# Transposes of the next chunk's keys and values placed between the state products of an mLSTM chunk on TensorE

## The chip, the cores and the metric

The kernel runs on one core of one Trainium2 chip. The metric is the device time of one execution in microseconds. Each of the runs shown is one execution on that core; the median of the runs is what a change is judged by.

## What is computed

A decoder trunk of two layers is run once, for a prompt group (16 meta tokens and 1024 prompt tokens) and a sample group (8 sequences of 4 tokens). Layer 0 is sliding-window attention, layer 1 an mLSTM block; both groups share the weights. The part that matters here is the chunkwise mLSTM cell of layer 1, for 4 heads of width 512. Per head and chunk the reference does this:

```
b = jnp.cumsum(fc, axis=1)
...
s = jnp.einsum('bthd,bjhd->btjh', qc, kc) * w_intra
num = jnp.einsum('btjh,bjhd->bthd', s, vc) + w_inter[..., None] * jnp.einsum('bthd,bhde->bthe', qc, C)
den = jnp.sum(s, axis=2) + w_inter * jnp.einsum('bthd,bhd->bth', qc, n)
h = num / jnp.maximum(jnp.abs(den), jnp.exp(-m_t))[..., None]
...
C_new = decay[..., None, None] * C + jnp.einsum('bjhd,bjhe->bhde', kc * wk[..., None], vc)
n_new = decay[..., None] * n + jnp.einsum('bjh,bjhd->bhd', wk, kc)
```

`s` are the scores of a chunk, `num` the numerator, `C` the 512x512 state and `n` the sum of keys. Outputs are the trunk's outputs and all new states, among them the 512x512 state of each head for the prompt and for each of the 8 sample sequences.

## The kernel before

The program has two blocks. The first does layer 0 and the projections of layer 1, and leaves queries, keys, values and two gate tensors in HBM (`scratch_q`, `scratch_k`, `scratch_v`, `scratch_ga`, `scratch_gb`). The second block (from about 1514 us of the span on) is the cell and the output projection, and holds the change. Each engine has its own program, in which the order is the order of the code; the engines meet in semaphores alone.

**Loops.** Each engine runs the four heads in turn. A head has 9 prompt chunks, c = 0 to 8: chunk 0 is the 16 meta tokens, the others have 128 tokens. The 8 sample sequences are taken along: iteration c of the chunk loop also does the state update of sequence c - 2. Behind the loop stand the last sequence, the samples' outputs and the output projection (L1813), and between its tiles the entry of the next head (its sample chunk and its chunk 0).

**An iteration on TensorE** (`cell_pe`, L1759 to L1797) has this order:

1. numerator and denominator from the old state (L1770, L1773), with the four state updates of sample sequence c - 2 between them (L1706), then the chunk's own part of both (L1776, L1781);
2. the state products: four products of keys and values, k = 0 to 3, each of three matmuls of 512 columns (high and low parts, L1788), which alternate between two PSUM banks. Product k waits until VectorE has added product k - 2 to the state (L2053, `c_done`);
3. `pre(c + 1)`: it waits until the next chunk's queries, keys and values have landed (`wait_chunk`) and until the two PSUM banks `KT_` and `VT_` are free, turns the keys (4 transposes) and the values (4 transposes; L1679), and multiplies keys and queries to scores (L1685);
4. the sample numerator of sequence c - 1 (L1716), and the transposes of chunk c's normed output (`back`, L1697), which wait for ScalarE (L1912).

VectorE has, in an iteration, the statistics of the numerator's rows (L2017), and between its small steps the four additions to the state (L2053), then the weighting of the next scores (L1961). ScalarE norms the output of chunk c (L1905 to L1912) before it copies the turned keys and values of chunk c + 1 out of PSUM (L1881, L1883). GpSimd scales the next chunk's queries (L1587), for which it too waits until the chunk has landed, and prepares the sample keys (L1605).

**Loads and stores** are all issued by SP, in one queue, in the order of `cell_sp` (L1541 to L1550). A chunk's three tensors (256 KB each) go into one of two buffers `chin`, which the next chunk but one uses again. From iteration 2 on the queue runs through this cycle, for b = c - 2:

```
            if b + 3 < NP:
                chunk_load(sp, h, b + 3)
                chunk_weights(sp, h, b + 3)
            sp.wait_ge(sem("c_done"), due(NU * h + u_samp(b, 3) + 1))
            sp.dma_start(state(o["sample_mlstm_c"], b), scs[b % 2][:, :, :]).then_inc(sem(f"sc_out{b % 2}"), 16)
            if b + 2 < DECB:
                state_load(b + 2)
            if b + 3 < NP:
                chunk_gates(sp, h, b + 3)
```

`state_load` waits until the store just issued (1 MB) has landed, since it loads the next sequence's state (1 MB) into the same buffer. Behind it come the gates (2 x 256 KB), and then the queries, keys and values of chunk c + 2. These are the ones that TensorE turns in iteration c + 1.

Of the kernel before, what the change touches and what calls it, by code (L numbers as in the profile page):

```python
# [42 lines left out]
P = 128  # L43
# [13 lines left out]
SR = 3 * NSM  # L57
# [31 lines left out]
def due(n):  # L89

    n = n.v if isinstance(n, Idx) else n
    return max(n, 0) if isinstance(n, int) else n
# [31 lines left out]
def build(nc, a, o):  # L124
# [3 lines left out]
    def sem(name):  # L128
        if name not in sems:
            sems[name] = nc.alloc_semaphore(name + sem_suffix[0])  # L130
        return sems[name]
# [22 lines left out]
    ident = const("ident", [P, P])  # L154
# [126 lines left out]
    NCH = NBLK + 2  # L281
# [22 lines left out]
    kv3 = rbuf("kv3", [P, 2, 4, SR])  # L304
# [1096 lines left out]
    NP = NBLK + 1  # L1401
# [34 lines left out]
    def pre_no(c):  # L1436

        return 0 if c == NCH - 1 else c + 1
# [9 lines left out]
    def chunk_in(c):  # L1448
        return smin if c == NCH - 1 else chin[c % 2]
# [5 lines left out]
    def wait_chunk(eng, h, c):  # L1455
        if c == NCH - 1:
            eng.wait_ge(sem("smin"), 144 * h + 144)
        else:
            eng.wait_ge(sem(f"chin{c % 2}"), due(48 * turn_of(h, c) + 48))
# [203 lines left out]
            cell_gp(gp, h + 1, entry=True)()  # L1663

    def cell_pe(pe, h, entry=False):
        def pre(c):

            n, x = ROWN[c], chunk_in(c)
            sample = c == NCH - 1
            wait_chunk(pe, h, c)  # L1670
            pe.wait_ge(sem("kv_ev"), due(2 * NCH * h + 2 * pre_no(c)))
            if c == 0:
                pe.wait_ge(sem("k3_lo"), 2 * h + 2)
            else:
                pe.wait_ge(sem("kv_lo"), due(2 * NP * h + (0 if sample else 2 * c)))
            for i, bank in ((1, KT_), (2, VT_)):
                for k in range(4):
                    src = kv3[:, i - 1, k, :] if sample else x[:, i, k, 0:n]
                    last = pe.transpose(bank[0:SR if sample else n, k * P:(k + 1) * P], src, ident[:, :])  # L1679
                last.then_inc(sem("kv_t"), 1)  # L1680
            pe.wait_ge(sem("sw_done"), due(NCH * h + pre_no(c)))
            pe.wait_ge(sem("small_read"), due(NZ * h + (c + 1 if 0 < c < NCH - 1 else 0)))
            for k in range(4):
                keys = kv3[:, 0, k, :] if sample else x[:, 1, k, 0:n]
                last = pe.matmul(score_bank(c)[0:SR if sample else n, 0:n], keys, x[:, 0, k, 0:n], start=(k == 0), stop=(k == 3))  # L1685
            last.then_inc(sem("s_done"), 1)
# [72 lines left out]
        for c in range(NP):  # L1759
            n, r = ROWN[c], c % 2  # L1760

            pe.wait_ge(sem("sw_done"), due(NCH * h + pre_no(c) + 1))
            wait_apart(pe, sem("kv_ev"), 2 * NCH * h + 2 * pre_no(c) + 2)
            pe.wait_ge(sem("h_done"), due(NCH * h + c))
            small(c + 1)
            if c > 0:
                pe.wait_ge(sem("qs_ready"), due(NCH * h + pre_no(c) + 1))
                pe.wait_ge(sem("c_done"), due(NU * h + u_tile(c - 1, 3) + 1))
                for k in range(4):
                    pe.matmul(pm[0][0:n, :], qs[r][:, k, 0:n], cst[:, k, :], start=(k == 0), stop=False)  # L1770
                    if k == 0:
                        pe.wait_ge(sem("nst_done"), due(NP * h + c))
                    pe.matmul(SM[0:n, 0:1], qs[r][:, k, 0:n], nst[:, k:k + 1], start=(k == 0), stop=False)  # L1773
                    if c > 1:
                        sample_update(c - 2, k)
            pe.matmul(SM[0:n, 0:1], swb[r][0:n, 0:n], ones[0:n, 0:1], start=(c == 0), stop=True)  # L1776
            wait_apart(pe, sem("sw_hi"), NP * h + c + 1)
            wait_apart(pe, sem("sw_lo"), NP * h + c + 1)
            wait_apart(pe, sem("kv_lo"), 2 * NP * h + 2 * c + 1)
            for i, (w, v) in enumerate(((swh, vh), (swh, vl), (swl, vh))):  # L1780
                last = pe.matmul(pm[0][0:n, :], w[r][0:n, 0:n], v[r][0:n, :], start=(c == 0 and i == 0), stop=(i == 2))  # L1781
            last.then_inc(sem("small_ready"), 1)
            pe.wait_ge(sem("kv_lo"), due(2 * NP * h + 2 * c + 2))
            for k in range(4):
                u = u_tile(c, k)
                pe.wait_ge(sem("c_done"), due(NU * h + u - 1))
                for i, (w, v) in enumerate(((kh, vh), (kh, vl), (kl, vh))):
                    last = pe.matmul(U_[u % 2], w[r][0:n, k * P:(k + 1) * P], v[r][0:n, :], start=(i == 0), stop=(i == 2))  # L1788
                last.then_inc(sem("u_ready"), 1)
            if c + 1 < NP:  # L1790
                pre(c + 1)
            if c >= 1:
                sample_numerator(c - 1)
            if c == NP - 1:
                for k in range(4):
                    sample_update(DECB - 1, k)
            back(c)  # L1797
# [939 lines left out]
```

## Time and profile before

| what | us |
|---|---|
| median of 3 runs | 2267.84 |
| lowest and highest of them | 2266.93, 2269.08 |
| the profiled execution, its own time | 2262.78 |
| its span | 2261.0 |
| TensorE busy in it | 2133.8 (94%) |
| VectorE, ScalarE, GpSimd busy in it | 1049.9, 768.1, 486.7 |
| mean granted clock of TensorE | 0.971 |

The span is the time from the first to the last instruction of the program; 1.8 us of the execution lie around it. The profiled execution is 5.1 us shorter than the median of the runs. Busy shares are means over stages that differ: the chunk loop of the cell, where the change is, takes about 105 us in each of the four heads, and only its own rows tell what ends which wait there. Matmuls are pipelined: a row's duration reaches from its start to its end, and the pitch from one start to the next is what it costs in a stream.

### The profile page before, as it was taken

How to read it: one execution, taken by the hardware profiler on the slowest of the kernel's cores; microseconds unless marked ns; L12 is line 12 of the kernel's file. 1: busy time of each engine (PE TensorE's matmuls, PEld its weight loads, DVE VectorE, ACT ScalarE, POOL GpSimd, SP SyncE). 2: the span in 40 equal slices, each digit the busy share in tenths (PEclk: the TensorE clock that was granted, in tenths of full speed). 3: DMA queues.
4: the chain of work that ended last, by engine and by line, in shares of the span. 5: the costliest groups of instructions: out<-in, count | busy, mean ns of one | idle time of the engine just before them, and what ended most of it. 6: DMA issues, size and time to landing. Idle time of an engine off the chain costs nothing. (4 is left out here: it accounts for less than half of the span.)

```text
span 2261.0 us, 32879 instructions
## 1 busy us (share of the span) xinstructions
PE 2133.8 (94%) x13089; PEld 1872.3 (83%) x13089; DVE 1049.9 (46%) x1843; ACT 768.1 (34%) x1609; POOL 486.7 (22%) x479
## 2 busy tenths in 40 slices
PE   4999979998999999999999999985989989989998
PEld 4999977777999989998999899974668668668668
DVE  6222247845645305431543054315753753753762
ACT  3114658843333222332323232313422421421431
POOL 3000015632420001000100010001531531531540
PEclk8999989999999999999999999996999999999999
DMA  6631122013631332233223322228764764664772
GB/s 220 76 88 38 38 58 71 1 32 119 177 88 60 113 125 68 67 115 122 62 66 121 120 61 69 105 80 236 241 190 142 223 207 143 208 215 130 216 226 79
DMA packets 321886, 272.20 MB, mean 120 GB/s; under 512 B 57958, under 2 KB 268454, under 8 KB 321651
## 3 DMA queue, kind: packets, MB, share of 16 engines
q1 hardware_dynamic: 307854, 221.58, 33.2%
q10 hardware_dynamic: 13880, 48.52, 6.6%
q8 instruction: 105, 1.72, 0.3%
q14 instruction: 47, 0.39, 0.1%
HBM read 168.89 MB, written 102.11 MB: 120 GB/s over the span
## 5 line engine op out<-in xcount | busy, mean ns | idle before, releaser
L369 ACT ACTIVATE sb_whi<-sb_wraw 128x1024 fp32r<-128x1024 f32 x108 | 114.1, 1058 | 455.5 <-PE ps L390 379.8
L374 DVE TENSOR_TENSOR sb_wlo<-sb_wraw,sb_whi 128x1024 fp32r<-128x1024 f32 x108 | 140.0, 1297 | 270.1 <-ACT sb_whi L369 263.8
L390 PE MATMUL ps<-sb_h1h,sb_whi 128*128 128x358 f32 x1152 | 252.9, 327 | 0.0
L390 PE MATMUL ps<-sb_h1h,sb_wlo 128*128 128x358 f32 x1152 | 252.8, 327 | 0.0
L390 PE MATMUL ps<-sb_h1l,sb_whi 128*128 128x358 f32 x1152 | 251.4, 326 | 0.0
L390 PEld LDWEIGHTS ps<-sb_h1h,sb_whi 128*128 128x128 f32 x1152 | 199.0, 189 | 2.0 <-issue 1.8
L390 PEld LDWEIGHTS ps<-sb_h1l,sb_whi 128*128 128x128 f32 x1152 | 199.2, 189 | 0.0
L390 PEld LDWEIGHTS ps<-sb_h1h,sb_wlo 128*128 128x128 f32 x1152 | 199.1, 189 | 0.0
L1049 POOL COPY sb_ctail<-sb_xr 128x3 f32<-128x3 f32 x16 | 3.0, 186 | 698.2 <-DVE sb_xr L1182 698.2
L1770 PE MATMUL pm<-sb_cst,sb_qs 128*128 128x512 f32 x256 | 133.4, 603 | 0.1
L390 PE MATMUL ps<-sb_hh,sb_whi 128*128 128x358 f32 x480 | 116.7, 352 | 15.8 <-DVE sb_hl L412 12.6
L1155 ACT ACTIVATE sb_st<-ps 128x1074 f32<-128x1074 f32 x48 | 51.2, 1067 | 222.7 <-PE ps L390 222.7
L1813 PE MATMUL ps<-sb_uh,sb_whi 128*128 128x358 f32 x384 | 93.6, 339 | 18.2 <-POOL sb_ul L1620 18.2
L390 PE MATMUL ps<-sb_hh,sb_wlo 128*128 128x358 f32 x480 | 107.3, 332 | 0.0
L390 PE MATMUL ps<-sb_hl,sb_whi 128*128 128x358 f32 x480 | 107.1, 332 | 0.0
L1976 DVE SCALAR_TENSOR_TENSOR sb_scs<-sb_scs,sb_hbc,ps 128x512 f32<-128x512 f32 x128 | 94.1, 742 | 26.7 <-PE ps L1706 26.7
L390 PEld LDWEIGHTS ps<-sb_hh,sb_whi 128*128 128x128 f32 x480 | 85.5, 194 | 24.7 <-issue 9.6
L1773 PEld LDWEIGHTS ps<-sb_nst,sb_qs 128*128 128x128 f32 x256 | 48.6, 190 | 62.2 <-issue 62.2
L2053 DVE SCALAR_TENSOR_TENSOR sb_cst<-sb_cst,sb_hbc,ps 128x512 f32<-128x512 f32 x128 | 91.8, 741 | 0.0
L1813 PE MATMUL ps<-sb_ul,sb_whi 128*128 128x358 f32 x384 | 91.0, 332 | 0.0
L1813 PE MATMUL ps<-sb_uh,sb_wlo 128*128 128x358 f32 x384 | 90.7, 332 | 0.0
L2176 DVE TENSOR_TENSOR sb_x1T<-ps,sb_x1T 128x1074 f32<-128x1074 f32 x32 | 40.9, 1277 | 104.5 <-PE ps L1813 104.5
(398 smaller groups left out, 4669.4 us busy)
## 6 DMA issues: line engine op xcount, KB each, us to landing
sb_scs<-state_mlstm_c SPq DMA_DIRECT2D x32, 1024.0 KB, 5.7
sample_mlstm_c<-sb_scs SPq DMA_DIRECT2D x32, 1024.0 KB, 4.9
sb_wraw<-mlstm_w_in SPq DMA_DIRECT2D x48, 512.0 KB, 3.9
sb_wraw<-swa_w_in SPq DMA_DIRECT2D x20, 512.0 KB, 3.8
scratch_ga<-sb_st ACTq DMA_DIRECT2D x16, 537.0 KB, 2.9
scratch_gb<-sb_st ACTq DMA_DIRECT2D x16, 537.0 KB, 4.3
scratch_v<-sb_st ACTq DMA_DIRECT2D x16, 537.0 KB, 2.9
scratch_q<-sb_st ACTq DMA_DIRECT2D x16, 537.0 KB, 2.8
```

What stands on the lines that cost most here:

```text
L369: act.activation(whi[q][:, :], wraw[q][:, :], ACT.Copy).then_inc(sem("w_hi"), 1)
L374: dve.tensor_tensor(wlo[q][:, :], wraw[q][:, :], whi[q][:, :].bitcast(F32), ALU.subtract)\
L390: last = pe.matmul(ps[s][:, g, 0:GRP], w[:, kk, c * P:(c + 1) * P], x[:, kk, g * GRP:(g + 1) * GRP], start=(kk == 0 and i == 0), stop=(kk ...
L1049: gp.tensor_copy(dst[:, 0:CW - 1], x[:, NPR:XPR])
L1155: act.activation(v3(st[b][:, 0, :]), ps[c][:, :, 0:GRP], ACT.Copy, scale=(MD ** -0.5 if i // 4 == 2 else 1.0)).then_inc(sem("qkv_ev"), 1)
L1770: pe.matmul(pm[0][0:n, :], qs[r][:, k, 0:n], cst[:, k, :], start=(k == 0), stop=False)
L1773: pe.matmul(SM[0:n, 0:1], qs[r][:, k, 0:n], nst[:, k:k + 1], start=(k == 0), stop=False)
L1813: last = pe.matmul(ps[i % 2][:, g, 0:GRP], w[:, k, c * P:(c + 1) * P], x[:, k, g * GRP:(g + 1) * GRP], start=(k == 0 and t == 0), stop=(k ...
L1976: dve.scalar_tensor_tensor(scs[b % 2][:, k, :], scs[b % 2][:, k, :], hbc[:, 1, NP + b:NP + b + 1], U_[u % 2], ALU.mult, ALU.add).then_inc( ...
L2053: ins = dve.scalar_tensor_tensor(cst[:, k, :], cst[:, k, :], hbc[:, 1, c:c + 1], U, ALU.mult, ALU.add)
L2176: dve.tensor_tensor(v3(x1T[:, i, :]), ps[i % 2][:, :, 0:GRP], v3(x1T[:, i, :]), ALU.add).then_inc(sem("o_done"), 1)
```

## The change

`pre` is taken apart into `turn(c, i)`, which turns the keys (i = 1) or the values (i = 2) of chunk c, and `multiply(c)`, the scores. `turn(c, 1)` carries the waits that stood at the head of `pre`: the one for the chunk's landing, and those for the two PSUM banks. In the chunk loop, the keys of chunk c + 1 are turned behind state product k = 1 of chunk c, its values behind product k = 2, and its scores follow product k = 3. The entry of a head (sample chunk and chunk 0) keeps its order. No instruction is added or taken away on any engine, and the code of the other engines is the same.

```diff
     def cell_pe(pe, h, entry=False):
+        def turn(c, i):
+
+            n, x, bank = ROWN[c], chunk_in(c), (KT_, VT_)[i - 1]
+            sample = c == NCH - 1
+            if i == 1:
+                wait_chunk(pe, h, c)
+                pe.wait_ge(sem("kv_ev"), due(2 * NCH * h + 2 * pre_no(c)))
+                if c == 0:
+                    pe.wait_ge(sem("k3_lo"), 2 * h + 2)
+                else:
+                    pe.wait_ge(sem("kv_lo"), due(2 * NP * h + (0 if sample else 2 * c)))
+            for k in range(4):
+                src = kv3[:, i - 1, k, :] if sample else x[:, i, k, 0:n]
+                last = pe.transpose(bank[0:SR if sample else n, k * P:(k + 1) * P], src, ident[:, :])
+            last.then_inc(sem("kv_t"), 1)
+
         def pre(c):
+
+            turn(c, 1)
+            turn(c, 2)
+            multiply(c)
+
+        def multiply(c):
...
@@ -1787,8 +1798,10 @@
                 for i, (w, v) in enumerate(((kh, vh), (kh, vl), (kl, vh))):
                     last = pe.matmul(U_[u % 2], w[r][0:n, k * P:(k + 1) * P], v[r][0:n, :], start=(i == 0), stop=(i == 2))
                 last.then_inc(sem("u_ready"), 1)
+                if c + 1 < NP and k in (1, 2):
+                    turn(c + 1, k)
             if c + 1 < NP:
-                pre(c + 1)
+                multiply(c + 1)
             if c >= 1:
                 sample_numerator(c - 1)
```

On TensorE, behind the numerator of an iteration, this is the order before (L1781 numerator, L1788 state products, L1679 transposes, L1685 scores, L1716 sample numerator):

```order
L1781 MATMUL pm<-sb_vh_222,sb_swl_214 128x512
L1788 MATMUL ps<-sb_vh_222,sb_kh_218 128x512
L1788 MATMUL ps<-sb_vl_224,sb_kh_218 128x512
L1788 MATMUL ps<-sb_vh_222,sb_kl_220 128x512
...
L1788 MATMUL ps<-sb_vh_222,sb_kl_220 128x512
L1679 MATMUL ps<-sb_ident,sb_chin_189 128x128 x8
L1685 MATMUL ps<-sb_chin_189 128x128 x4
L1716 MATMUL ps<-sb_scs_205,sb_qz 32x512 x4
```

All eight transposes stand behind the twelfth matmul of the state products; the lines left out are the other products.

The same place in the changed kernel, from product k = 1 on (its lines are L1799 for the state products, L1679 for the transposes, L1696 for the scores, L1727 for the sample numerator):

```order
L1799 MATMUL ps<-sb_vh_222,sb_kl_220 128x512
L1679 MATMUL ps<-sb_ident,sb_chin_189 128x128 x4
L1799 MATMUL ps<-sb_vh_222,sb_kh_218 128x512
L1799 MATMUL ps<-sb_vl_224,sb_kh_218 128x512
L1799 MATMUL ps<-sb_vh_222,sb_kl_220 128x512
L1679 MATMUL ps<-sb_ident,sb_chin_189 128x128 x4
L1799 MATMUL ps<-sb_vh_222,sb_kh_218 128x512
L1799 MATMUL ps<-sb_vl_224,sb_kh_218 128x512
L1799 MATMUL ps<-sb_vh_222,sb_kl_220 128x512
L1696 MATMUL ps<-sb_chin_189 128x128 x4
L1727 MATMUL ps<-sb_scs_205,sb_qz 32x512 x4
```

The first four transposes, with the wait for the landing, moved up past two products, the other four past one.

## Rows read from the trace of the kernel before

**Rows 1.** Timeline of TensorE, head 0, iteration 3 (start, duration, [idle before])
```profile
1601.14 0.40 PE L1788 MATMUL ps<-sb_vh,sb_kh 128*128 128x512 f32 x1
...
1602.29 0.39 PE L1788 MATMUL ps<-sb_vh,sb_kl 128*128 128x512 f32 x1
1602.84 0.50 PE L1788 MATMUL ps<-sb_vh,sb_kh 128*128 128x512 f32 x1 [0.16 <-DVE sb_cst L2053]
...
1604.37 1.03 PE L1679 MATMUL ps<-sb_ident,sb_chin 128*128 128x128 f32 x8
1605.24 1.06 PE L1685 MATMUL ps<-sb_chin 128*128 128x128 f32 x8
```
**Rows 2.** Timeline of all engines, same iteration and the start of the next
```profile
1606.32 0.59 ACT L1883 ACTIVATE sb_vh<-ps 128x512 fp32r<-128x512 f32 x1
1607.71 1.02 PE L1770 MATMUL pm<-sb_cst,sb_qs 128*128 128x512 f32 x2
```
**Rows 3.** Who waited for whom, whole span, GpSimd (total us, times, longest us)
```profile
POOL sb_qs L1587 <- DMA sb_chin<-scratch_v: 66.3, 21, 4.5
```
**Rows 4.** Timeline of TensorE, head 0, iteration 7
```profile
1655.44 1.09 PE L1679 MATMUL ps<-sb_ident,sb_chin 128*128 128x128 f32 x8
1656.38 1.06 PE L1685 MATMUL ps<-sb_chin 128*128 128x128 f32 x8
```
**Rows 5.** Timelines of GpSimd and SP, head 0, iterations 3 to 8
```profile
1603.00 1.29 POOL L1587 TENSOR_TENSOR sb_qs<-sb_chin,sb_wnt 128x512 f32<-128x512 f32 x1 [2.53 <-DMA sb_chin<-scratch_v]
...
1613.95 0.38 SPq L1546 DMA_DIRECT2D sample_mlstm_c<-sb_scs  x1
...
1628.71 1.30 POOL L1587 TENSOR_TENSOR sb_qs<-sb_chin,sb_wnt 128x512 f32<-128x512 f32 x1 [2.74 <-DMA sb_chin<-scratch_v]
...
1639.43 0.38 SPq L1546 DMA_DIRECT2D sample_mlstm_c<-sb_scs  x1
...
1655.47 1.27 POOL L1587 TENSOR_TENSOR sb_qs<-sb_chin,sb_wnt 128x512 f32<-128x512 f32 x1 [4.02 <-DMA sb_chin<-scratch_v]
...
1665.09 8.14 SPq L1546 DMA_DIRECT2D sample_mlstm_c<-sb_scs  x2
```
**Rows 6.** The same of head 2, iterations 3 to 8
```profile
1945.76 1.29 POOL L1587 TENSOR_TENSOR sb_qs<-sb_chin,sb_wnt 128x512 f32<-128x512 f32 x1 [2.40 <-DMA sb_chin<-scratch_v]
...
1956.85 0.38 SPq L1546 DMA_DIRECT2D sample_mlstm_c<-sb_scs  x1
...
1973.37 1.27 POOL L1587 TENSOR_TENSOR sb_qs<-sb_chin,sb_wnt 128x512 f32<-128x512 f32 x1 [4.49 <-DMA sb_chin<-scratch_v]
...
1982.99 0.38 SPq L1546 DMA_DIRECT2D sample_mlstm_c<-sb_scs  x1
...
1999.46 1.28 POOL L1587 TENSOR_TENSOR sb_qs<-sb_chin,sb_wnt 128x512 f32<-128x512 f32 x1 [4.38 <-DMA sb_chin<-scratch_v]
...
2009.07 8.14 SPq L1546 DMA_DIRECT2D sample_mlstm_c<-sb_scs  x2
```
**Rows 7.** The same of head 3, iterations 7 and 8
```profile
2174.00 1.28 POOL L1587 TENSOR_TENSOR sb_qs<-sb_chin,sb_wnt 128x512 f32<-128x512 f32 x1 [3.69 <-DMA sb_chin<-scratch_v]
...
2183.78 0.38 SPq L1546 DMA_DIRECT2D sample_mlstm_c<-sb_scs  x1
```
**Rows 8.** Timeline of TensorE, head 1, iteration 0 (first matmul of product k = 2)
```profile
1737.04 0.49 PE L1788 MATMUL ps<-sb_vh,sb_kh 16*128 16x512 f32 x1
```
**Rows 9.** Chain that ended last, head 0, iteration 0
```profile
1560.40 5.12 PE ps L1788 x12
```
**Rows 10.** Timeline of TensorE behind head 0's chunk loop
```profile
1676.92 0.96 PE L1813 MATMUL ps<-sb_uh,sb_whi 128*128 128x358 f32 x2 [2.60 <-POOL sb_ul L1620]
1688.89 0.43 PE L1813 MATMUL ps<-sb_uh,sb_whi 128*128 128x358 f32 x1 [1.95 <-POOL sb_ul L1620]
```
**Rows 11.** Busy time by stretch, same place (columns PE, PEld, DVE, ACT, POOL, then PEclk, DMA share, GB/s)
```profile
1676.90:1680.30 3.40, 3.38 (x11) 3.38 (x12) 0.00 (x0) 0.75 (x1) 0.00 (x0) 0.50 1.02 352
1686.90:1690.30 3.40, 1.45 (x9) 1.41 (x9) 0.29 (x1) 0.31 (x1) 0.90 (x2) 1.00 0.09 13
```

More of the change, by code:

```diff
@@ L1665, in cell_pe @@
     def cell_pe(pe, h, entry=False):
+        def turn(c, i):
[12 more added lines that the diff above has]
+            last.then_inc(sem("kv_t"), 1)
         def pre(c):
+            turn(c, 1)
+            turn(c, 2)
+            multiply(c)
+        def multiply(c):
             n, x = ROWN[c], chunk_in(c)
             sample = c == NCH - 1
[L1670 to L1680, printed above, removed]
             pe.wait_ge(sem("sw_done"), due(NCH * h + pre_no(c)))
```

## The prediction

> **What bounds the kernel now.** I read the chunk loop as TensorE's timeline first. In iteration 3 of head 0 the state products start at 1601.14, and the last matmul of product k = 1 starts at 1602.29 [rows 1]. With the pitch of 0.23 in that stream (five pitches from 1601.14 to 1602.29) product 1 is through at 1602.52, so two products take 1.38. Product 2 starts only at 1602.84, released by VectorE's addition to the state. The transposes follow at 1604.37 and the scores at 1605.24: eight transposes take 0.87, and products 2 and 3 take 1.53 where an unhindered pair takes 1.38. TensorE is thus the bound, apart from small stalls between its state products. From the end of product 1 to the scores it takes 2.72.
>
> The second view is what else ends near there. GpSimd scales the next chunk's queries when the chunk's load has landed. It waited for that landing 21 times, 66.3 us in all [rows 3], in iteration 3 of head 0 until 1603.00 [rows 5]. So the chunk lands there about 0.5 **behind** the end of product 1, and 1.4 ahead of the place where TensorE asks for it now. In iteration 7 it lands so late that TensorE waits for it even now: its transposes start at 1655.44, GpSimd at 1655.47 [rows 4, 5]. That pair ties the two clocks: TensorE can start 0.03 before the GpSimd row.
>
> **What the change does to an iteration.** It moves 8 transposes per iteration in 8 iterations of 4 heads; nothing is added. If the chunk has landed, product 1 is followed by keys 0.43, product 2 0.69, values 0.43, product 3 0.69: 0.87 + 1.38 = 2.25, against 2.72. Product 2 is then due at 1602.95, behind the release of 1602.84, so VectorE's stall is filled. **Gain: 0.47 per iteration** whose chunk has landed in time. What hides the rest: ScalarE copies keys and values only behind its norm of chunk c, and starts the values' copy at 1606.32, done 1606.91; TensorE's next iteration starts at 1607.71, at 1607.24 once it is 0.47 earlier, still behind that copy [rows 2]. If that cover went, up to 0.3 of the gain would go. The scores' bank and VectorE's last addition stand where they did relative to TensorE.
>
> The moved wait is the other half. Behind it on TensorE now stand products 2 and 3, which used to fill the time until the landing. SP's queue is touched only through its waits: the load of the next chunk but one is issued behind the landing of the store of the sample state, and this store is issued when GpSimd's and TensorE's sample update of the iteration is through. I therefore take the landing in iteration c as a fixed time behind the store of iteration c - 1. It is 1628.71 - 1613.95 = 14.76 in head 0, iteration 5, 16.04 in its iteration 7, and 16.52 and 16.47 in head 2, by GpSimd's rows [rows 5, 6].
>
> **A late turn costs** from the landing: the eight transposes started on a landing took 0.94 instead of 0.87 (1655.44 to 1656.38 [rows 4]), plus two products at 0.69, 2.32 in all; and from the scores (1605.24) to the next store (1613.95) 8.71 [rows 1, 5]. So the next store comes 2.32 + 8.71 - 0.03 = 11.00 behind GpSimd's row of the landing. This makes a chain in hops of two chunks: store of iteration 2, landing in 3, store in 4, landing in 5, store in 6, landing in 7, store in 8. Each hop, before any shift is carried along, moves its store by landing + 11.00 minus the store's time now:
>
> - Head 0: 1603.00 gives +0.05, 1628.71 gives +0.28, 1655.47 gives +1.38, in sum +1.71 [rows 5].
> - Head 2: -0.09, +1.38, +1.39, in sum +2.68 [rows 6].
> - Heads 1 and 3 by the same subtraction (twelve pairs in all, the last 2174.00 and 2183.78, +1.22 [rows 7]): +1.08 and +1.59.
>
> Together +7.06. Against this stand the gains ahead of the chain, in iterations 0 and 1, whose loads are issued long before. In iteration 1 it is 0.47 in each head. In iteration 0 it depends on the clock: head 0 runs it at half clock without a stall (twelve matmuls in 5.12, 0.43 each [rows 9]), so nothing is gained, and head 3 I take the same; in heads 1 and 2 products are stalled as elsewhere (product 2 starts at 1737.04 [rows 8]) and I take 0.33, the stall alone. Sum of the gains: 4 x 0.47 + 2 x 0.33 = 2.54. The gain of iteration 2 does not count, since the landing in 3 hangs on the store of 2, which is issued before its turn. **Net: +7.06 - 2.54 = +4.5 us.**
>
> On the profiled execution that is 2262.78 + 4.5 = 2267.3. The median of the runs is 5.1 above that execution, and the forecast is made for a median: 2267.84 + 4.5, rounded down to **2272**, because a store that is issued earlier against the rest of the loads may leave the last landings a little sooner.
>
> **Bounds of the unknown.** How the time from store to landing moves when the cycle is shifted, no row shows. From below I take 14.76, the shortest of the four shown, for every hop in iterations 5 and 7 that is longer now: that takes back about 6.5 and gives -2, 2265.8. From above, all eight of these hops at 16.5 add about 7.6: +12, 2280. I keep the present values, between the two, since these very transfers have them.
>
> **Rivals.**
>
> *The landings follow TensorE.* If the loads had slack that the shortened iterations would use, all turns would be on time: 28 x 0.47 + 2 x 0.33 = 13.8, 2254. For it speaks that a store is issued as soon as its update is through. Against it speaks that the landing is late by 0.5 to 2 in iterations 3 to 7 of every head and hangs on a chain of transfers that TensorE doesn't shorten. Chance 0.08. A middle way, in which the landings come 0.5 to 1 sooner per hop, takes 6 to 12 from the sum: -1.5 to -7.5, 2260 to 2266. Chance 0.18, of which 0.12 lie below 2263.3.
>
> *The clock falls in the new waits.* The turns in iteration 7 will leave TensorE idle for about 2 in a piece (in head 0 product 1 of iteration 3 ends at 1602.52 and stores follow each other at 12.74, (1639.43 - 1613.95) / 2 [rows 5], so product 1 of iteration 7 ends near 1602.52 + 4 x 12.74 = 1653.48, 1.96 ahead of 1655.44 [rows 4]). In the trace an idle piece of 1.95 left the granted clock at 1.00; behind one of 2.60 the stretch from 1676.90 stood at 0.50, that is 1.2 instead of 2.4 GHz [rows 10, 11]. The new idle pieces lie near the first of the two. Each such fall costs, by that stretch, half of 3.4, 1.7. Once per head it makes +6.8 on top, 2279; in all late turns, 18 or so, +30. It decides from idle pieces over 1.95 on. The forecast holds with none. Chance 0.10. The Trainium skill, "TensorE: Matmul & The Clock Gate", section "Why this matters for your kernels", advises against idle gaps between bursts of matmuls, because the clock goes back to half; it speaks against moving a DMA wait to where nothing is left to fill it. With its rule at work the sum would be that of this rival, without it that of the forecast; the piece of 1.95 above went without a fall.
>
> *The fill is worth nothing either way.* Late turns lose just what the early ones gain: 2268. This is the forecast with hops shorter by 0.4 each, and its chance is in the cases above and below.
>
> **How the numbers follow.** A difference below 0.2%, 4.5 us, can't be told from none here. Forecast (landing chain as it is), 0.62: its own range is 2268 to 2277, and its middle lies on that border, so 0.30 of it count as the same and 0.32 as slower. Landings on time 0.08, faster. Landings somewhat sooner 0.18: 0.12 faster, 0.06 the same. Clock 0.10, slower. What is left, 0.02, is the same. In sum faster 0.20, same 0.38, slower 0.42. The range that holds 8 in 10 leaves out the full gain, and the clock falling in many turns: 2259 to 2280.
>
> **What the changed profile would show.** Right if: the transposes of the keys (L1679) wait for the landing of `scratch_v` in some 18 of 20 turns of iterations 3 to 7, 15 to 20 us in all, where they hardly wait now; the state products no longer wait for VectorE; the store of iteration 3 follows that of iteration 2 at 12.3 instead of 12.74; from iteration 3 on the spacing is uneven and 12.7 to 13.3 on average, and the store of iteration 8 in each head is 0.4 to 2 later against the head's start than now. The time from store to landing stays at 14.5 to 16.5. Wrong if the spacing stays at 12.3 up to iteration 8 (landings on time), if waits vanish because stores land sooner, if ScalarE's copies of the values become what the numerator waits for, or if the granted clock shows 0.5 in the chunk loop behind iteration 0.

## The result and the profile after

The changed kernel takes 2293.41 us (median of 6 runs, 2283.29 to 2297.32), the kernel before beside it 2268.46 (6 runs, 2266.25 to 2276.93). The ratio, here and below that of the means of the runs, is 1.0096, with a 95% interval of 1.0075 to 1.0117: some 22 us slower (the two medians lie 25.0 apart). The forecast was 2272, the range ended at 2280. Slower was the likeliest of the three signs, at 0.42; the size was far off.

The profiled execution of the changed kernel has a span of 2291.3 us, against 2261.0, and TensorE's mean clock is 0.961, against 0.971. The page of the profile (busy time; then the chain that ended last, by engine and by line) reads:

```profile
PE 2153.4 (94%) x13089; PEld 1885.1 (82%) x13089; DVE 1057.4 (46%) x1843; ACT 769.5 (34%) x1609; POOL 486.6 (21%) x479
...
PE 21%; DMA 6%; DVE 3%; SPq 1%; POOL 1%; issue 1%; ACT 0%; POOLq 0%; DVEq 0%
PE ps L1826 9%; PE pm L1781 4%; DMA sb_chin<-scratch_v 3%; DMA sample_mlstm_c<-sb_scs 2%; PE ps L1799 2%; PE ps L1679 2%; PE ps L1696 1%; PE ps L1717 1%; DVE sb_scs L1989 1%; PE ps L1727 1%; SPq L1480 1%; PE pm L1708 1%; SPq L1495 1%; PE pm L1792 1%; PE ps L1784 0%
```

TensorE is busy 19.6 us longer, with the same 13,089 matmuls. A wait alone would not make it busier; a lower clock does. And the loads of the values and the stores of the sample state now have 5% of the span on the chain between them, where the page of before had 1% for each. The waits of the whole span say what waits for the landing:

```profile
POOL sb_qs L1587 <- DMA sb_chin<-scratch_v: 64.0, 21, 4.0
...
PE ps L1679 <- DMA sb_chin<-scratch_v: 16.6, 17, 1.8
```

GpSimd waits as before (66.3 us, [rows 3]); TensorE's transposes wait 16.6 us, where the trace of before has 0.7.

**Where the 30.3 us of span lie.** I cut the cell of both traces at the first state product of each iteration:

| stretch, sum over four heads | before | after | difference |
|---|---|---|---|
| up to the cell's first state product | 1560.2 | 1568.2 | +8.0 |
| iteration 0 to iteration 1 | 55.8 | 71.2 | +15.4 |
| iteration 1 to iteration 3 | 101.9 | 98.3 | -3.6 |
| iteration 3 to iteration 8 | 256.4 | 267.0 | +10.7 |
| iteration 8 to the next head, or to the end of the span | 286.7 | 286.6 | -0.1 |

The first row is no effect of the change: the code there is the same, and in the profiles of the experiments below it lies anywhere from 1560.1 to 1570.5, in either order of the cell. The rest is 22.3, close to the 22 of the ratio, though each trace is one execution. Two thirds of it lie in iteration 0, which the prediction had costed at a gain.

**Iteration 0.** These are TensorE's rows of head 1 in the changed kernel, from the entry and the first state product of iteration 0 to the first product of iteration 1, and the busy time by stretch in the same place (columns as in [rows 11]):

```profile
1750.00 0.20 PE L1787 MATMUL ps<-sb_ones,sb_swb 16*16 16x1 f32 x2 [1.37 <-DVE sb_x1T L2189]
...
1750.84 0.39 PE L1799 MATMUL ps<-sb_vh,sb_kh 16*128 16x512 f32 x1
...
1752.35 1.11 PE L1679 MATMUL ps<-sb_ident,sb_chin 128*128 128x128 f32 x4
1753.39 0.79 PE L1799 MATMUL ps<-sb_vh,sb_kh 16*128 16x512 f32 x1
1753.99 0.62 PE L1799 MATMUL ps<-sb_vl,sb_kh 16*128 16x512 f32 x1
...
1757.59 2.08 PE L1696 MATMUL ps<-sb_chin 128*128 128x128 f32 x8
1759.59 0.60 PE L1708 MATMUL pm<-sb_ident,sb_hb 16*128 16x16 f32 x4
...
1768.30 0.39 PE L1799 MATMUL ps<-sb_vh,sb_kh 128*128 128x512 f32 x1
```

```profile
1752.20:1765.80 13.60, 13.60 (x37) 8.39 (x37) 4.88 (x15) 6.07 (x19) 4.77 (x6) 0.50 0.27 74
1765.80:1769.20 3.40, 3.40 (x16) 2.37 (x15) 0.70 (x3) 0.00 (x0) 0.30 (x1) 0.99 0.43 111
```

The same place of the kernel before:

```profile
1734.52 0.20 PE L1776 MATMUL ps<-sb_ones,sb_swb 16*16 16x1 f32 x2 [1.37 <-DVE sb_x1T L2176]
...
1735.35 0.39 PE L1788 MATMUL ps<-sb_vh,sb_kh 16*128 16x512 f32 x1
...
1738.84 1.97 PE L1679 MATMUL ps<-sb_ident,sb_chin 128*128 128x128 f32 x8
1740.60 1.60 PE L1685 MATMUL ps<-sb_chin 128*128 128x128 f32 x8
1742.13 0.42 PE L1697 MATMUL pm<-sb_ident,sb_hb 16*128 16x16 f32 x4
...
1747.93 0.40 PE L1788 MATMUL ps<-sb_vh,sb_kh 128*128 128x512 f32 x1
```

```profile
1738.30:1741.70 3.40, 3.40 (x16) 2.87 (x15) 1.26 (x2) 2.84 (x6) 0.00 (x0) 0.50 0.00 0
1741.70:1745.10 3.40, 3.36 (x17) 2.13 (x17) 2.14 (x6) 1.99 (x5) 1.88 (x3) 0.99 0.13 27
```

In both, the clock goes to half (1.2 instead of 2.4 GHz) at the entry of the head, behind a wait of 1.37 and in the products of 16 rows that follow it, or at their end. Before, it stood at half for 3.4 us, in which the eight transposes and the scores ran in one piece, and then it was back. In the changed kernel it stands at half for 13.7 us, in this head and in heads 2 and 3. The two falls do not come at the same place: 2.97 behind the first product before, 1.37 behind it after; what that does is taken up with the table of iteration 0 below. From the first product to `back` it takes 8.75 instead of 6.78 (1759.59 - 1750.84, 1742.13 - 1735.35), and from there to the next first product 8.71 instead of 5.80: there the same matmuls run, until 1765.8 at half clock. The head's iteration 0 takes 17.46 instead of 12.58 us.

**The turns in the chunk loop.** TensorE's rows of head 0, a turn in time (iteration 1) and a late one (iteration 3), transposes of the keys and scores:

```profile
1588.46 0.60 PE L1679 MATMUL ps<-sb_ident,sb_chin 128*128 128x128 f32 x4
...
1590.73 1.05 PE L1696 MATMUL ps<-sb_chin 128*128 128x128 f32 x8
...
1614.31 0.66 PE L1679 MATMUL ps<-sb_ident,sb_chin 128*128 128x128 f32 x4 [1.09 <-DMA sb_chin<-scratch_v]
...
1616.63 1.05 PE L1696 MATMUL ps<-sb_chin 128*128 128x128 f32 x8
```

Landings and stores of head 0, from the store of iteration 2 on, which answer to [rows 5]:

```profile
1599.43 0.38 SPq L1546 DMA_DIRECT2D sample_mlstm_c<-sb_scs  x1
1611.73 0.38 SPq L1546 DMA_DIRECT2D sample_mlstm_c<-sb_scs  x1
1614.33 1.28 POOL L1587 TENSOR_TENSOR sb_qs<-sb_chin,sb_wnt 128x512 f32<-128x512 f32 x1 [3.33 <-DMA sb_chin<-scratch_v]
...
1625.34 0.38 SPq L1546 DMA_DIRECT2D sample_mlstm_c<-sb_scs  x1
...
1641.06 1.29 POOL L1587 TENSOR_TENSOR sb_qs<-sb_chin,sb_wnt 128x512 f32<-128x512 f32 x1 [3.70 <-DMA sb_chin<-scratch_v]
1652.07 0.38 SPq L1546 DMA_DIRECT2D sample_mlstm_c<-sb_scs  x1
...
1668.12 1.29 POOL L1587 TENSOR_TENSOR sb_qs<-sb_chin,sb_wnt 128x512 f32<-128x512 f32 x1 [4.03 <-DMA sb_chin<-scratch_v]
1679.13 8.14 SPq L1546 DMA_DIRECT2D sample_mlstm_c<-sb_scs  x2
```

From landing to store it is 11.01 in all three hops (1625.34 - 1614.33 and so on). From store to landing it is 14.90, 15.72 and 16.05; before it was 14.54, 14.76 and 16.04.

### The profile page after: what moved, and what is told of

Same layout as the page of the kernel before. It is cut to its first block and busy times, and to the rows that moved or that the text cites. A ratio compares the mean times of both kernels' runs of the same rounds, so it can differ in the third digit from the quotient of the medians.

```text
span 2291.3 us, 32879 instructions
## 1 busy us (share of the span) xinstructions
PE 2153.4 (94%) x13089; PEld 1885.1 (82%) x13089; DVE 1057.4 (46%) x1843; ACT 769.5 (34%) x1609; POOL 486.6 (21%) x479
## 5 line engine op out<-in xcount | busy, mean ns | idle before, releaser
L1781 PE MATMUL pm<-sb_cst,sb_qs 128*128 128x512 f32 x256 | 140.9, 633 | 0.0
L390 PE MATMUL ps<-sb_hh,sb_whi 128*128 128x358 f32 x480 | 117.4, 354 | 15.1 <-DVE sb_hl L412 12.0
L1826 PE MATMUL ps<-sb_uh,sb_whi 128*128 128x358 f32 x384 | 93.6, 339 | 16.8 <-POOL sb_ul L1620 16.8
L2066 DVE SCALAR_TENSOR_TENSOR sb_cst<-sb_cst,sb_hbc,ps 128x512 f32<-128x512 f32 x128 | 94.4, 744 | 24.6 <-PE ps L1799 24.6
L1613 POOL TENSOR_TENSOR sb_ub<-sb_ub,sb_chga 128x512 f32<-128x512 f32 (+1 forms) x36 | 41.9, 1165 | 238.7 <-DVE sb_ub L2076 238.7
```

Of the source, the lines that this page charges most:

```text
L390: last = pe.matmul(ps[s][:, g, 0:GRP], w[:, kk, c * P:(c + 1) * P], x[:, kk, g * GRP:(g + 1) * GRP], start=(kk == 0 and i == 0), stop=(kk ...
L1613: gp.tensor_tensor(u[:, :, 0:n], u[:, :, 0:n], gb[:, :, 0:n], ALU.add).then_inc(sem("u_add"), 1)
L1826: last = pe.matmul(ps[i % 2][:, g, 0:GRP], w[:, k, c * P:(c + 1) * P], x[:, k, g * GRP:(g + 1) * GRP], start=(k == 0 and t == 0), stop=(k ...
L2066: ins = dve.scalar_tensor_tensor(cst[:, k, :], cst[:, k, :], hbc[:, 1, c:c + 1], U, ALU.mult, ALU.add)
```

## The experiments

Each ratio is to runs of the kernel before on the same chip as the run, whose median was 2270.7 to 2272.1 us; not all experiments ran on the same chip, so two of them are compared by their ratios. Where I give a stage from one profiled execution, that execution is only one sample.

**Iteration 0 apart from the rest.** The first kernel is the changed one with the old order in iteration 0:

```diff
-                if c + 1 < NP and k in (1, 2):
+                if c + 1 < NP and c > 0 and k in (1, 2):
                     turn(c + 1, k)
             if c + 1 < NP:
-                multiply(c + 1)
+                (multiply if c > 0 else pre)(c + 1)
```

> The changed kernel with iteration 0 of each head back in the old order (transposes behind all four state products), the new order in iterations 1 to 7. Theory A (clock): the new order in iteration 0 mixes 16-row products and transposes, which keeps TensorE at half clock for 10 to 14 us where the dense run of transposes and scores ended it after 3 to 10; then iteration 0 goes back from 17.4 to 12.6 to 15.2 us in heads 1 to 3 and the total falls by 10 to 17 against the changed kernel, to about 1.003 of the kernel before. Theory B (landings alone): the loss is that of the late turns in iterations 3 to 7, and iteration 0 was an accident of the profiled execution; then the total stays near 1.009 of the kernel before.

Measured: 2282.93, ratio 1.0049 [1.0029, 1.0070]. That is some 10.5 us below the changed kernel, as the theory of the clock had it; the loss that is left is the theme of the runs on late turns below.

The second has the new order in iteration 0 alone (`c == 0` in both conditions):

> The kernel before with the new order in iteration 0 of each head alone. Theory A (clock): 10 to 17 us slower than the kernel before, 1.005 to 1.007, with half clock over 13.65 us in iteration 0. Theory B (landings): within 2 us of the kernel before.

Measured: 2280.62, ratio 1.0047 [1.0029, 1.0064]. The two halves add up to the whole, 1.0096. Iteration 0 alone, in which every chunk has landed and nothing waits for a load, costs about 10.7 us. Its profile shows where: iteration 0 takes 65.3 us in the four heads instead of 55.8, with head 1 at half clock for 10.2 us.

```profile
1743.80:1754.00 10.20, 10.20 (x32) 6.49 (x31) 4.89 (x17) 4.11 (x10) 0.53 (x2) 0.50 0.00 0
1754.10:1757.50 3.40, 3.40 (x13) 1.81 (x12) 0.52 (x1) 1.86 (x10) 3.24 (x5) 1.00 0.82 203
```

The other half, iterations 1 to 7, costs about 11 us where the sum had 5.2 (7.06 - 1.88). In the profile of the first kernel the clock fell three times inside the chunk loops, at late turns, twice in head 0 and once in head 3 (after a wait of 2.25). Those of head 0:

```profile
1610.12 0.66 PE L1679 MATMUL ps<-sb_ident,sb_chin 128*128 128x128 f32 x4 [2.03 <-DMA sb_chin<-scratch_v]
...
1638.89 1.11 PE L1679 MATMUL ps<-sb_ident,sb_chin 128*128 128x128 f32 x4 [2.36 <-DMA sb_chin<-scratch_v]
```

```profile
1611.00:1614.40 3.40, 3.40 (x15) 2.98 (x14) 1.49 (x2) 1.42 (x3) 1.98 (x2) 0.55 0.28 31
1638.90:1642.30 3.40, 3.40 (x13) 2.95 (x14) 0.75 (x1) 1.59 (x3) 2.83 (x2) 0.54 0.47 183
```

That is the rival of the clock, at work in this execution. With such a fall it takes 12.5 to 12.6 us from the landing to the next store, where it is 11.0 in the late turns without one: 1.5 to 1.6 us each. A wait of 2.48 in this trace, at 1667.66, brought no fall, so no point between can be read from these rows. In the profile of the change itself no wait at a turn is over 1.80 us, and the clock does not fall between the first state products of iterations 1 and 8 of any head.

**Turns in time and late turns apart.** New order in iterations 1 and 2 alone (`c in (1, 2)`), where the chunk has landed, but for iteration 1 of head 0, where TensorE's turn waited 0.95 for it:

> The new order in iterations 1 and 2 of each head alone, where the chunk has landed long before. All theories: 0.45 us per iteration are gained by filling the stall between state products, eight times; the second one of each head is partly given back if the landing in iteration 3 is waited for even in the old order, which it is not. 3.6 us faster, 0.9984. If the fill itself is worth nothing, 1.000.

Measured: 2272.95, ratio 1.0007 [0.9996, 1.0018]. The miss is of use. The profile has the gain, 24.6 us for the two iterations instead of 25.5 in three of four heads (25.8 in head 0, with its wait), and then from iteration 3 to iteration 8 it has 64.5 to 65.6 instead of 63.8 to 65.0: 4.7 us more in sum. The store of iteration 2 came earlier, and the load behind it took longer:

```profile
1594.71 0.38 SPq L1546 DMA_DIRECT2D sample_mlstm_c<-sb_scs  x1
...
1610.34 1.09 PE L1679 MATMUL ps<-sb_ident,sb_chin 128*128 128x128 f32 x8
1610.37 1.29 POOL L1587 TENSOR_TENSOR sb_qs<-sb_chin,sb_wnt 128x512 f32<-128x512 f32 x1 [4.09 <-PE ps L1799]
```

By GpSimd's rows it is 15.66 us from this store to the landing in iteration 3, and before 14.54 (1603.00 - 1588.46); in heads 1 to 3 it is 14.50, 14.46 and 15.80, against 14.22, 14.40 and 14.88. Time won ahead of a landing is lost at the landing.

New order from iteration 3 on alone (`c > 2`), where the chunk is late:

> The new order in iterations 3 to 7 of each head alone, where the landing is behind the end of product 1. If the parts add up, it is e1_first_old plus 3.6 us: the waits for the landing stand against the fill, 11 to 14 us slower than the kernel before, 1.005 to 1.006, with waits of keys for the landing in about 18 of 20 turns. The hop sum of the prediction, without a fall of the clock, wants 7 us, 1.003. If late turns cost nothing: 1.000.

Measured: 2283.49, ratio 1.0046 [1.0030, 1.0061]. Within the intervals, the late turns carry the whole of the 11 us. In this profile the clock fell at waits of 1.88, 2.12 and 2.39 us, and stayed up at one of 2.33. The three turns with a fall took 12.4 to 12.6 us from the landing to the next store, the late ones without it 11.0.

**The loads ahead of the state load.** If the late landing is the cause, the same order must gain once the landing is early. SP issues the queries, keys and values of the chunk after next right behind the store, ahead of the state load that waits for this store; iteration 0 keeps the old order:

```diff
+        chunk_load(sp, h, 3)
+        chunk_weights(sp, h, 3)
         for b in range(DECB):
-            if b + 3 < NP:
-                chunk_load(sp, h, b + 3)
-                chunk_weights(sp, h, b + 3)
             sp.wait_ge(sem("c_done"), due(NU * h + u_samp(b, 3) + 1))
             sp.dma_start(state(o["sample_mlstm_c"], b), scs[b % 2][:, :, :]).then_inc(sem(f"sc_out{b % 2}"), 16)
+            if b + 4 < NP:
+                chunk_load(sp, h, b + 4)
+                chunk_weights(sp, h, b + 4)
             if b + 2 < DECB:
                 state_load(b + 2)
```

> New order in iterations 1 to 7, old order in iteration 0, and SP issues the loads of chunk c + 2 right behind the store of the sample state instead of behind the next state's load and the gates. Theory A and the landing theory: no turn waits for a landing any more, and 28 x 0.45 = 12.6 us are gained against the kernel before: 0.9945. If the landings were not what cost, the total is that of the kernel with iteration 0 old and SP unchanged.

Measured: 2256.66, ratio 0.9935 [0.9918, 0.9952]: 14.8 us faster than the kernel before, and the best version of this study. Head 0's stores and GpSimd's scaling:

```profile
1597.60 0.38 SPq L1545 DMA_DIRECT2D sample_mlstm_c<-sb_scs  x1
...
1609.13 1.29 POOL L1589 TENSOR_TENSOR sb_qs<-sb_chin,sb_wnt 128x512 f32<-128x512 f32 x1
...
1609.89 0.38 SPq L1545 DMA_DIRECT2D sample_mlstm_c<-sb_scs  x1
```

In iterations 3 to 7 no wait for the landing is left (one of 0.84 is, in iteration 1 of head 0), by GpSimd's row the chunk has landed 11.53 us behind the store, the stores follow each other at 12.29, and from iteration 3 to iteration 8 each head takes 61.5 instead of 63.8 to 65.0.

Is it SP's order alone? The same edit to SP, with the kernel before's TensorE:

> The kernel before, in its own order on TensorE, with SP issuing the loads of chunk c + 2 right behind the store of the sample state. Landing theory: in the old order only a few turns wait for the landing (under 3 us in all), so 0 to 3 us faster, 0.9987 to 1.000. The rival, that SP's order alone makes e5's gain of 14 us, wants 0.9935.

Measured: 2267.24, ratio 0.9984 [0.9965, 1.0002]. No: with the old order TensorE is hardly reached by the late landing (0.7 us of waits in all), so an earlier one is worth little; the interval takes in no change at all. And the new order in all iterations, with SP's edit:

> The changed kernel as it is, iteration 0 included, with SP issuing the loads of chunk c + 2 right behind the store. It differs from e5_loads_early by the order in iteration 0 alone. Clock theory: 10 to 15 us slower than e5_loads_early, so about 1.000 of the kernel before, with half clock over some 13 us in iteration 0. Without the clock theory: 0.9935 as e5_loads_early.

Measured: 2264.04, ratio 0.9970 [0.9956, 0.9984]. From iteration 3 to iteration 8 it runs as the best version does, 61.5 per head; what lies between the two (7.4 us by the medians, with intervals of the ratios that do not meet) is iteration 0, this time with no late landing anywhere near.

**Another filling.** The sample numerator, which needs no load, between products k = 1 and k = 2 of the kernel before:

```diff
                 last.then_inc(sem("u_ready"), 1)
+                if c >= 1 and k == 1:
+                    sample_numerator(c - 1)
             if c + 1 < NP:
                 pre(c + 1)
-            if c >= 1:
-                sample_numerator(c - 1)
```

> The kernel before, with the sample numerator of the iteration (four matmuls that wait for no landing of this iteration) between state products k = 1 and k = 2, and keys, values and scores of the next chunk where they were. Clock and landing theory: the stall ahead of product 2 is filled in iterations 1 to 8 without an earlier wait for the landing and without touching iteration 0; 32 x 0.45 = 14 us to gain if the landings allow it. They are 14 to 17 us behind the store of the iteration before, and the turn would be asked for 16 us behind it, so some turns wait: 6 to 14 us faster, 0.994 to 0.9975. If the stall between the products were not worth filling: 1.000.

Measured: 2274.33, ratio 1.0016 [1.0001, 1.0031]. With SP's edit added:

> As e6_numerator, with SP issuing the loads of chunk c + 2 right behind the store of the sample state. No turn waits for a landing: 32 x 0.45 = 14.4 us faster than the kernel before, 0.9937, and 1.8 us faster than e5_loads_early, since iteration 8 has the fill too. If e5's gain came from SP's order alone, it is the same as e8_before_loads.

Measured: 2269.80, ratio 0.9993 [0.9979, 1.0007]. Both miss: an iteration takes 12.57 even without any wait for a load, where 12.29 was expected. TensorE's rows of the second, head 0:

```profile
1632.70 0.40 PE L1790 MATMUL ps<-sb_vh,sb_kl 128*128 128x512 f32 x1
1633.03 1.06 PE L1718 MATMUL ps<-sb_scs,sb_qz 128*32 128x512 f32 x8
1634.03 0.50 PE L1790 MATMUL ps<-sb_vh,sb_kh 128*128 128x512 f32 x1
1634.37 0.40 PE L1790 MATMUL ps<-sb_vl,sb_kh 128*128 128x512 f32 x1
```

The numerator starts 0.33 behind the last product's start, and the product behind it is followed at 0.34, where the pitch is 0.23: about 0.1 for each change of the kind of matmul. That covers most of the missing 0.28; the rest I did not follow. Iteration 0 is old in both, yet in the profile of the second it takes 15.1 in all four heads, with half clock for 10.2 us in heads 1 to 3. That the clock of iteration 0 differs between kernels which have the same code there limits what one profile can say of it, and the medians have to carry it.

**What in iteration 0 costs.** Three kernels change iteration 0 of the kernel before alone. Keys and values turned together behind product k = 1, the scores behind k = 3:

```diff
                 last.then_inc(sem("u_ready"), 1)
+                if c == 0 and k == 1:
+                    turn(c + 1, 1)
+                    turn(c + 1, 2)
             if c + 1 < NP:
-                pre(c + 1)
+                (multiply if c == 0 else pre)(c + 1)
```

> The kernel before, with iteration 0 of each head alone changed: keys and values of chunk 1 are turned in one piece behind state product k = 1, and the scores stay behind product k = 3. Theory A1: the clock stays at half because the dense stretch of 128-row transposes and scores, which ended it in the kernel before, is broken up by 16-row products; here it is broken once (the scores stand apart) instead of twice: iteration 0 between the old 12.6 to 15.2 and the new 14.3 to 17.5 us, the total 2 to 8 us above the kernel before. Theory A2: the loss in iteration 0 comes from the switches between transposes and products at half clock (about 0.5 us each): one pair of switches instead of two, 1 to 2 us in the four heads, 1.000 to 1.001.

Measured: 2280.02, ratio 1.0037 [1.0023, 1.0052]. These are 8 us; A1 had 2 to 8, A2 1 to 2. Breaking the sequence once costs nearly what breaking it twice does (1.0047, and the intervals overlap), so the number of changes between 16-row products and transposes is not what sets the cost.

The whole of `pre(1)`, transposes and scores in one piece, behind product k = 1 (`if c == 0 and k == 1: pre(c + 1)`, and the old place for c > 0 only):

> The kernel before, but in iteration 0 of each head the whole of pre(1) (eight transposes and the scores, in one piece) stands behind state product k = 1; the products k = 2 and 3 of 16 rows follow it. Theory D (the half clock ends soon where eight transposes and the scores stand together, wherever they are): half clock of 3 to 7 us at heads 1 and 2 in the profile, time within 0.999 to 1.002 of before. Theory E (what counts is that nothing of 16 rows stands behind or between them, products of 16 rows behind them keep the clock down): half clock of 10 to 14 us per head as in the run with keys and values together, ratio 1.003 to 1.005.

Measured: 2277.57, ratio 1.0030 [1.0012, 1.0047]. The keys alone behind product k = 1, values and scores together behind k = 3:

> The kernel before, but in iteration 0 of each head the four transposes of the keys alone stand behind state product k = 1; the values' four and the scores stay together behind product k = 3. Theory D (the dense piece of transposes and scores has to be whole): four transposes missing from it are enough, ratio 1.003 to 1.005 and half clock of 10 us and more at heads 1 and 2. Rival (a shorter dense piece behind all products still brings the clock back): ratio 1.000 to 1.0015 and half clock of 3.4 to 7 us.

Measured: 2277.70, ratio 1.0027 [1.0014, 1.0040]. Busy time by stretch of the first of these two, head 1:

```profile
1744.70:1751.40 6.70, 6.70 (x24) 5.31 (x24) 2.69 (x9) 2.33 (x6) 0.00 (x0) 0.50 0.00 0
1751.50:1754.80 3.30, 2.52 (x12) 1.67 (x12) 2.37 (x7) 1.11 (x3) 0.45 (x2) 1.00 0.00 0
1754.90:1758.20 3.30, 3.30 (x8) 1.81 (x7) 1.01 (x2) 2.24 (x12) 3.14 (x5) 0.50 0.73 190
```

and of the second, heads 1 and 3:

```profile
1745.00:1755.10 10.10, 10.10 (x34) 7.39 (x33) 4.50 (x14) 3.11 (x8) 0.00 (x0) 0.50 0.00 0
...
2103.30:2113.50 10.20, 10.20 (x30) 6.46 (x29) 3.44 (x8) 6.03 (x19) 4.84 (x6) 0.50 0.38 100
```

With the piece whole, the clock does come back at the end of it, at 1751.4, and falls again 3.4 us later, behind the last two products of 16 rows and a wait of 0.78; so it is in heads 0 and 2 too, but in head 3 the half clock lasts 13.7 us in one piece. With four transposes taken out of it, it lasts 10.2 us in heads 1 and 3 and 13.7 in head 2. In the first run both theories are half right: as D has it, the half clock ended where the dense piece stood, in three heads of four, and as E has it, the time is lost all the same; whether the second fall comes of the 16-row products or of the wait of 0.78 was not told apart. The second run came out as D has it. Iteration 0 by kernel:

| kernel | iteration 0, sum of four heads, us | half clock in heads 1, 2, 3, us | ratio of the whole kernel |
|---|---|---|---|
| before | 55.8 | 3.4, 3.4, 10.2 | 1 |
| loads early, old order there | 56.4 | 10.2, 3.4, 6.8 | 0.9935 |
| keys alone inside | 66.3 | 10.2, 13.7, 10.2 | 1.0027 |
| whole of pre inside | 65.6 | 6.8 + 3.4, 6.8 + 3.4, 13.7 | 1.0030 |
| turned together inside | 66.6 | 13.7, 10.2, 10.2 | 1.0037 |
| new order there alone | 65.3 | 10.2, 6.8, 13.7 | 1.0047 |
| loads early, new order everywhere | 65.3 | 10.2, 13.7, 6.8 | 0.9970 |
| the change | 71.2 | 13.7, 13.7, 13.7 | 1.0096 |

Six profiles with the old order there lie at 55.8 to 57.1, those of the moved numerator at 57.7 and 60.5; the six with something of `pre(1)` between the products at 65.3 to 71.2.

**The place of the fall.** The length of the half clock also follows the place at which the clock falls, counted from the first product of iteration 0, and this place differs between executions of the same code. Heads 1 to 3 of the eight profiles with the old order there, and of the three with the new order (the change, new order there alone, loads early with new order everywhere):

| the fall, us behind the first product | half clock in the old order (cases) | in the new order (cases) |
|---|---|---|
| -0.4 to 0.4 | 10.2 (10) | 13.7 (2) |
| 0.5 to 0.8 | 6.8 (2), 10.2 (1) | 10.2 (2) |
| 1.2 to 1.4 | 6.8 (3) | 13.7 (3) |
| 2.9 to 3.2 | 3.4 (8) | 6.8 (2) |

At a like place the new order has 3.4 to 6.9 us more of half clock in every row but the second, where one old case has as much. Head 0 comes to iteration 0 at half clock already; there it ends 8.2 to 11.2 us behind the first product in the eight old profiles and 14.5 to 16.8 us behind it in the three new ones. This also sizes the rival of A2: at the same 10.2 us of half clock iteration 0 takes 14.9 to 15.2 us in the old order and 15.4 to 15.7 where a part of `pre(1)` stands between the products, so what the order costs beside the clock is under 1 us per head. And it says why the profile of the change (71.2) lies above those of the same order elsewhere (65.3): its three falls came at 1.37, 0.24 and 0.10, places of 13.7 us each. The keys alone inside had 13.7 and 10.2 us where the old order has 6.8 and 3.4 (falls at 1.20 and 3.00); its head 1, shown above, fell at the first product, where the old order has 10.2 as well.

## Why the prediction was wrong

- **A turn in time: right.** Priced at 2.25 from the end of product 1 to the scores; the rows have 2.27 (1590.73 - 1588.46). The stores of iterations 2 and 3 follow at 12.30 (1611.73 - 1599.43), as said, and VectorE's stall is gone but in iteration 8, which has the old order.
- **A late turn: right.** Priced at 2.32 from the landing to the scores, and 11.00 to the next store; the rows have 2.32 and 11.01. TensorE's wait for it was put at 15 to 20 us in 18 of 20 turns; it is 16.6 in 17.
- **The chain of landings: right in its mechanism, somewhat too small.** From the store of iteration 2 to that of iteration 8:

| head | before | after | more | predicted |
|---|---|---|---|---|
| 0 | 76.63 | 79.70 | +3.07 | +1.71 |
| 1 | 76.50 | 78.54 | +2.04 | +1.08 |
| 2 | 77.71 | 79.16 | +1.45 | +2.68 |
| 3 | 76.49 | 78.80 | +2.31 | +1.59 |
| sum | | | +8.87 | +7.06 |

  The time from store to landing in the three hops, which the sum held at its old values, is longer by 1.33, 0.90 and 0.69 in heads 0, 1 and 3, and shorter by 1.25 in head 2, +1.67 in sum. Without that the sum is 7.20, against 7.06. It was named as the unknown, and its bounds held it.
- **The gains of iterations 1 and 2: there, as said.** The two take 98.3 instead of 101.9. That their loads have landed long before is not so in head 0: there TensorE waits for the chunk of iteration 1, 0.95 in the kernel with the new order in iterations 1 and 2 alone and 0.84 in the one with early loads and the old iteration 0. The second of them buys nothing: the landing in iteration 3 hangs on the store of iteration 2, which the sum had too.
- **Iteration 0: this step failed.** The prediction said "in iteration 0 it depends on the clock", held head 0 and head 3 at nothing gained and took 0.33 each in heads 1 and 2, -0.66 in sum. It took the clock of before as given, as something that the order of the matmuls would meet but not move. It is +15.4 in the profile, about 10.7 by the run with iteration 0 alone, and 7.4 by the two kernels with early loads. The order of these matmuls sets, together with the place of the fall, how long the clock stays at half; the 15.4 of the one profile has bad luck with these places in it. The trace of before had a sign of it: half clock in head 0 was read as a fixed state of the stage [rows 9], and what brought it back was never asked.
- **The rival of the clock: the right engine, and the main loss in another place.** It looked for falls in new waits of about 2 us in the chunk loop. They do occur: three in the profile of the run with iteration 0 old, three in that of the late turns alone, at waits of 1.88 to 2.39 where the rival had them from 1.95 on. In the profile of the change there is none in iterations 1 to 7, and the loss at half clock lies in iteration 0. Since iterations 1 to 7 cost 11 us by the ratio, but 7.0 in the profiled execution of the change (10.65 - 3.63), such falls, at some 1.5 us each, may make up the rest in some executions; the runs do not show how often, and longer landings are a part of it too. That the forecast held with no falls was not secured by the two idle pieces that it leaned on: the trace of before has a wait of 2.60 at 1849.06, in head 1, with the clock at 1.00 behind it, and the trace of the change one of 1.95 at 1702.86 with 0.50 from 1704.4 on. The rule of the Trainium skill that the prediction weighed ("TensorE: Matmul & The Clock Gate", "Why this matters for your kernels"), against idle gaps between bursts, bears on these falls. In iteration 0 TensorE had no gap for as long as the clock stood at half; the only one is the wait of 1.37 ahead of it, which both kernels have.
- **The rival of landings in time** was the better description of what the order can be worth: 28 gains of 0.47 are 13.2, and the kernel with early loads and an old iteration 0 gains 14.8 (10.9 to 18.6 by the interval). It needs SP's order changed, which this change does not do.

What stays open: what exactly in the sequence of iteration 0 lets the clock come back. Shown is that it came back within 3.4 to 6.8 us in 13 of 24 later heads where eight transposes and eight score matmuls of 128 rows stood together behind all products (eight profiles) and never later than 10.8 us behind the first product, and that its half-clock stretches came to 10 us or more in 16 of 18 where products of 16 rows stood between or behind them. Whether the transposes, the scores or the rows of the operands count was not told apart. Also open is why falls came at waits of 1.88, 2.03, 2.12, 2.25, 2.36 and 2.39 us and not at those of 2.33 and 2.48. A kernel with `pre(1)` ahead of all products was not tried: by the code its scores wait for a step of VectorE that stands behind the first two additions to the state, so the two engines would wait for each other.

## What to carry to other kernels

A move that gains 0.47 us by filling a stall can put the wait for a load ahead of the work that used to hide it; before moving it, compare the landing with the new place, and if it is late, move the load first: here one and the same order on TensorE made the kernel 0.5% slower or 0.65% faster, by SP's order alone. Where an engine's clock changes in or near the stage that is edited, the clock is part of the price: look for what ran just before it came back, and keep that piece whole and behind the small matmuls. And exempt the iterations that differ from the rest (a short first chunk here) from a change that is made for the others.

## What the runs showed of the hardware

- At the head's entry the granted clock goes from 1.00 to 0.50 behind a wait of 1.37 us, in or near matmuls of 16 rows. How long it stays there depends on what follows and on where it falls: with a dense piece of transposes and scores behind the products it was 3.4 us when it fell 3.0 us behind the first product and 10.2 us when it fell near it; in all three later heads of the change it was 13.7 us, with TensorE busy 13.60 of 13.60 us in head 1. Being busy without a gap did not bring it back.
- At waits of 1.88 to 2.39 us inside a stream at full clock the clock fell to about half for 3.4 us in six cases; at other waits of 2.33 and 2.48 it did not. A like wait can cost 0 or some 1.5 us on top (12.4 to 12.6 from landing to store instead of 11.0). In the output projection a wait of 2.60 left the clock at 1.00 in head 1 of the trace of before; in head 0 it stood at 0.50 behind one.
- From the issue of the 1 MB store to the landing of the chunk behind it, through the state load, the gates and the chunk's tensors, it took 14.2 to 16.6 us before and 14.3 to 16.1 after, and up to 17.3 in the kernel with new order in iterations 1 and 2: it moves by 2 us and more with what else is under way when the store is issued.
- A change between state products and the sample numerator cost about 0.1 us on either side, which ate most of a gain of 0.47 per iteration.
